# Expert outputs written to a row per token and rank, and eight ranks summed at the end, in place of a scatter that accumulates

## The chip, the cores and the metric

The kernel runs on one core of one Trainium2 chip. The metric is the device time of one execution in microseconds (us). Three runs of the kernel before gave 1620.14, 1620.84 and 1623.35 us; the median is 1620.84 us.

A core has TensorE (PE, matmuls; its weight loads are shown as PEld), VectorE (DVE), ScalarE (ACT), GpSimd (POOL) and SyncE (SP, which here only issues DMAs). The tile memory (SBUF) has 128 partitions; matmuls write to PSUM, eight banks of 128 x 512 float32.

## The reference, cut to what matters

The layer is a token mixer (four kinds of attention) and a mixture of experts. The mixer is not touched by the change. 512 tokens of width 1024 are routed to 8 of 64 experts each:

```python
_, idx = lax.top_k(jnp.where(emask, choice, -jnp.inf), TOP_K)      # 8 experts per token
sel = jnp.take_along_axis(scores, idx, axis=1)
wts = sel / jnp.sum(sel, axis=-1, keepdims=True) * ROUTED_SCALE
...
yb = swiglu(x_pad[tok], w_gate_e[e], w_up_e[e], w_down_e[e]) * w[:, None]   # per expert
acc = acc.at[tok].add(yb)                                          # summed per token
...
x = layer_norm(ALPHA * x + shared + routed, ln2_g, ln2_b)
```

So each token's output is the sum of eight weighted expert outputs, a shared expert's output and the scaled residual, and then a second layer norm. There are 512 x 8 = 4096 pairs of token and expert, 64 per expert on average.

## The kernel before, in words

The program is written by hand for each engine, with semaphores between them. It has four stages: the mixer (to about 690 us), the output projection with first norm, router and shared expert (to about 820 us), the loop over the 64 experts (to 1580 us), and the final sum with the second norm.

The router makes a table `info[:, t, e, :]` per token tile t: the token number minus 65536 (`UNUSED`) and the token's weight for expert e. `pos` holds the slot of each token in each expert. For an expert there are 128 slots. DVE compares the slot numbers with `pos` (`mark_slots`), which gives a one-hot matrix, and PE multiplies it with `info` (`slots`, four matmuls, accumulated in bank I). The result is, per slot, a token number and a weight; an empty slot gives 0. `rows_of` on DVE adds 65536 and writes two row numbers: `rows_u[:, b, 0:1]` for the gather (an empty slot is 65536, out of bounds, and is skipped), and `rows_u[:, b, 1:2]` for the scatter, cut down by `min` to a spare row 512 + slot for an empty slot.

The expert loop runs four experts per turn of a hardware loop. GpSimd gathers the tokens' rows of `x1_d` (DRAM) to `x_slots`; PE turns them (L852), multiplies by the gate and up weights (L773), turns the hidden values, and multiplies by the down weights in three products of split float32 (L786, L787, L790). ACT and DVE scale half of the result each with the slots' weights to `y_slots` (L1079, L1421), and GpSimd scatters `y_slots` with an indirect DMA that accumulates (`compute_op=ALU.add`) to `acc_d[yb]`, one of two buffers of 640 rows in DRAM. GpSimd clears both buffers before the loop (L1543). SP loads each expert's 2 MB of gate and up weights and 1 MB of down weights one expert ahead, as the buffers come free.

The order on GpSimd in the loop is: gather for expert e+2 (needs `rows_made`, and the turned slots of e), then scatter of e (needs both halves of `y_slots`). `rows_out[b]` counts the scatters of each buffer.

After the loop, SP waits for `rows_out[0]` and issues four loads of 512 KB from `acc_d[0]`, then waits for `rows_out[1]` and issues four more (L552). DVE adds `acc[0]` to the base (`mT_nat(t)`, which already holds residual and shared expert; L1475), then per token tile t `total(t)` adds `acc[1]` (L1460) and takes mean and variance, and `scale(t)` normalises and multiplies by `ln2`'s gain (L1470, L1471). GpSimd takes the root (L1507) and adds the bias (L1594), and SP stores the tile (L555). The order on DVE is total(0), total(1), scale(0), total(2), scale(1), total(3), scale(2), scale(3). PE does nothing after the loop.

If an expert has more than 128 tokens, a slow branch handles the rest (`if n > P`); it isn't taken here, the profile has 64 scatters and 66 gathers.

Of the kernel before, what the change touches and what calls it, by code (L numbers as in the profile page):

```python
# [30 lines left out]
ALU = mybir.AluOpType  # L31
# [39 lines left out]
X_PARTS = 4  # L71
W_OUT_AFTER = N_PROJ + 26
# [103 lines left out]
def build(nc, a, out):  # L176
# [9 lines left out]
    with ctx:  # L186
# [40 lines left out]
        ov_slot = sb("ov_slot", [P, P])  # L227

# [55 lines left out]
        info, o = carve(region2, o, (QT, N_EXP + 2, 2))  # L284
# [5 lines left out]
        ln2, o = carve(region2, o, (2, D))  # L290
# [5 lines left out]
        acc = [w.rearrange("p a b -> p (a b)").rearrange("p (a b) -> p a b", a=QT) for w in w_gu]  # L296
# [24 lines left out]
        acc_d = [nc.dram_tensor(f"acc_d{b}", (SEQ + P, D), F32).ap() for b in range(2)]  # L321
# [97 lines left out]
        acc_in = [[sem(f"acc_in{b}_{t}") for t in range(QT)] for b in range(2)]  # L419
# [14 lines left out]
        def _(sp):  # L434
# [113 lines left out]
            sp.wait_ge(y_out1, 3 * QT)  # L548
            for b in range(2):
                sp.wait_ge(rows_out[b], 16 * (N_EXP // 2 + 1))  # L550
                for t in range(QT):
                    sp.dma_start(acc[b][:, t, :], acc_d[b][t * P:(t + 1) * P, :]).then_inc(acc_in[b][t], 16)  # L552
# [8 lines left out]
        def _(pe):  # L561
# [232 lines left out]
            def slots(j, b):  # L794

                pe.wait_ge(onehot_made, j + 1)
                pe.wait_ge(rows_made, j)
                for t in range(QT):
                    mm = nc.tensor.matmul(PS[:, I_BANK, 0:2], onehot[:, b % 2, t, :],  # L799
                                          info[:, t, bass.ds(j, 1), :].rearrange("p a b -> p (a b)"),  # L800
                                          start=(t == 0), stop=(t == QT - 1))
                mm.then_inc(slots_done, 1)
# [84 lines left out]
            with pe.If(n > P):  # L887
                pe.sem_inc(ov["y"], 1)
                with pe.Fori(1, SEQ // P) as c:
                    with pe.Fori(0, N_EXP) as e:  # L890
                        j = (c - 1) * N_EXP + e
                        pe.wait_ge(ov["oh"], j + 1)
                        for t in range(QT):
                            mm = nc.tensor.matmul(PS[:, I_BANK, 0:2], onehot[:, 0, t, :],
# [24 lines left out]
                        mm.then_inc(ov["y"], 1)  # L919

# [181 lines left out]
        def _(dve):  # L1102
# [173 lines left out]
            def route(t):  # L1276
# [20 lines left out]
                s = sel[:, t, :]  # L1297
                link(nc.vector.tensor_tensor_reduce(rt64[:, 3, :], s, score[:, :], 1.0, 0.0, ALU.mult, ALU.add,
# [3 lines left out]
                link(nc.vector.tensor_scalar(info[:, t, 0:N_EXP, 1], rt64[:, 3, :], wsum[:, 1:2], ROUTED_SCALE,  # L1302
                                             ALU.mult, ALU.mult))

            def slots_of(t):
# [15 lines left out]
                                         ALU.add))  # L1321
            first_norm(0)
# [45 lines left out]
            def rows_of(b, done):  # L1368
                nc.vector.tensor_copy(w_slot[:, b, :], PS[:, I_BANK, 1:2])
                row = PS[:, I_BANK, 0:1]  # L1370
                nc.vector.tensor_scalar(rows_u[:, b, 0:1], row, UNUSED, None, ALU.add)
                nc.vector.tensor_scalar(rows_u[:, b, 1:2], row, UNUSED, tok_row[:, QT:QT + 1], ALU.add, ALU.min)\  # L1372
                    .then_inc(done, 1)
# [111 lines left out]
        def _(pool):  # L1485
# [60 lines left out]
            last_row = pool.to_reg(SEQ + P - 1)  # L1546
# [96 lines left out]
```

## Time and profile before

| | before |
|---|---|
| median of the runs | 1620.84 us |
| profiled execution, its own time | span 1620.6 us from first to last instruction |
| PE busy | 1415.9 us, 87% of the span |
| DVE / ACT / POOL busy | 43% / 30% / 22% |
| moved by DMA | 319.95 MB, of it 55.60 MB on GpSimd's queue |
| HBM | read 290.21 MB, written 46.92 MB |

The page gives for each engine the busy time, then the span in 40 slices of 40.5 us, then DMA queues, the chain of work that ended last (each piece followed back to what released it), groups of instructions by line, and DMA issues. A busy share is an average over the whole span; the rows further down are taken from single stages. PEclk is the granted clock of TensorE as a share of full speed: 1.00 is 2.4 GHz and 0.50 is 1.2 GHz. A float32 matmul appears as two records (for 512 columns, two of about 0.43 us at full clock).

### The profile page before, as it was taken

What the parts mean: (1) busy time and instruction counts of PE and PEld (TensorE: products, weight loads), DVE (VectorE), ACT (ScalarE), POOL (GpSimd) and SP (SyncE); (2) the same over time, 40 slices, a digit from 0 to 9 for tenths busy, and PEclk for the clock granted to TensorE, in tenths of its full rate; (3) what the DMA queues carried; (4) which work ended last, traced back from release to release, by engine and by line L of the source; (5) the groups of instructions that cost most, each with busy time, mean ns of one, the idle gap of its engine ahead of it and who ended that gap; (6) DMA issues with size and microseconds to landing.
All of it is one profiled execution on the core that took longest, in us unless ns stands there. A gap on an engine that the chain in (4) does not pass through costs nothing.

```text
span 1620.6 us, 20567 instructions
## 1 busy us (share of the span) xinstructions
PE 1415.9 (87%) x7132; PEld 1143.1 (71%) x7132; DVE 701.0 (43%) x1620; ACT 487.3 (30%) x983; POOL 354.8 (22%) x236
## 2 busy tenths in 40 slices
PE   8500399999999899997899999999999999999990
PEld 5500389966666567645778888888888888888880
DVE  3000010156466555556444444545444444544446
ACT  4000132333333232101033433434343433434330
POOL 3000132222123234301011222212122221222224
PEclk9755699999999999997999999999999999999995
DMA  4222511111111114234269999999999999999974
GB/s 150 25 25 36 160 66 65 50 50 65 33 50 49 49 66 185 80 142 190 110 225 323 351 322 341 328 334 336 322 349 312 342 333 335 334 320 344 325 237 140
DMA packets 64768, 319.95 MB, mean 197 GB/s; under 512 B 10652, under 2 KB 10780, under 8 KB 56404
## 3 DMA queue, kind: packets, MB, share of 16 engines
q1 hardware_dynamic: 44692, 263.76, 43.4%
q0 software_dynamic: 20032, 55.60, 16.2%
q8 instruction: 28, 0.46, 0.1%
q14 instruction: 16, 0.13, 0.0%
HBM read 290.21 MB, written 46.92 MB: 208 GB/s over the span
## 4 chain that ended last, share of the span: by engine, by line
PE 81%; SPq 8%; DMA 5%; DVE 4%; issue 1%; ACT 1%; POOL 0%; POOLq 0%; DVEq 0%; ACTq 0%
PE PS L773 27%; PE PS L604 15%; PE PS L786 5%; SPq L467 4%; PE PS L787 4%; PE PS L852 4%; PE PS L790 4%; PE PS L730 3%; PE PS L799 3%; PE PS L712 3%; SPq L471 3%; PE PS L660 3%; PE PS L683 2%; DMA ring<-in_w_proj 2%; DMA slots<-x_d,rows_u 2%; PE PS L671 2%
## 5 line engine op out<-in xcount | busy, mean ns | idle before, releaser
L773 PE MATMUL PS<-region,slots 128*128 128x256 f32 x2048 | 454.0, 380 | 1.4 <-ACT slots L1053 1.4
L773 PEld LDWEIGHTS PS<-region,slots 128*128 128x128 f32 x2048 | 389.7, 190 | 57.0 <-issue 1.6
L1515 POOL TENSOR_TENSOR w_lo<-ring,w_hi 128x1024 fp32r<-128x1024 f32 x54 | 128.3, 2377 | 453.0 <-ACT w_hi L935 453.0
L604 PE MATMUL PS<-x_hi,w_hi 128*128 128x512 f32 x368 | 102.4, 422 | 125.2 <-ACT w_hi L935 125.2
L1551 POOL DMA_INDIRECT slots<-x_d,rows_u x66 | 68.9, 1044 | 606.6 <-DVE rows_u L1372 597.1
L604 PEld LDWEIGHTS PS<-x_hi,w_hi 128*128 128x128 f32 x368 | 69.4, 197 | 142.4 <-issue 129.4
L1168 DVE CUSTOM_DVE_ANT_0 region<-PS,region 128x128 f32<-128x128 f32 (+1 forms) x64 | 30.6, 478 | 309.8 <-PE PS L660 307.8
L1341 DVE TENSOR_TENSOR wd_lo<-region,wd_hi 128x1024 fp32r<-128x1024 f32 x130 | 153.5, 1222 | 23.9 <-ACT wd_hi L1033 23.9
L1033 ACT ACTIVATE wd_hi<-region 128x1024 fp32r<-128x1024 f32 x130 | 129.5, 1048 | 0.0
L1024 ACT ACTIVATE slots<-PS 128x128 f32<-128x128 f32 x136 | 37.9, 279 | 302.3 <-PE PS L773 302.3
L786 PE MATMUL PS<-wd_hi,hT_hi 128*128 128x512 f32 x272 | 119.5, 439 | 3.1 <-ACT hT_hi L1028 3.1
L1326 DVE TENSOR_TENSOR slots<-PS,slots 128x128 f32<-128x128 f32 x136 | 39.2, 288 | 190.7 <-ACT slots L1024 190.7
L1557 POOL DMA_INDIRECT acc_d<-slots,rows_u x64 | 103.2, 1613 | 52.9 <-DVE slots L1421 39.0
L787 PE MATMUL PS<-wd_lo,hT_hi 128*128 128x512 f32 x272 | 107.0, 394 | 0.0
L935 ACT ACTIVATE w_hi<-ring 128x1024 fp32r<-128x1024 f32 x54 | 56.7, 1049 | 140.6 <-DMA ring<-in_w_proj 139.8
L604 PE MATMUL PS<-x_hi,w_lo 128*128 128x512 f32 x376 | 95.5, 396 | 0.0
L604 PE MATMUL PS<-x_lo,w_hi 128*128 128x512 f32 x368 | 91.9, 392 | 0.0
L1334 DVE TENSOR_TENSOR hT_lo<-PS,hT_hi 128x128 fp32r<-128x128 f32 x136 | 38.9, 286 | 121.5 <-ACT hT_hi L1028 121.5
L979 ACT ACTIVATE region<-region,nmax 128x128 f32<-128x128 f32 (+3 forms) x80 | 43.6, 546 | 149.5 <-DVE nmax L1168 149.2
L790 PE MATMUL PS<-wd_hi,hT_lo 128*128 128x512 f32 x272 | 84.6, 392 | 0.0
L1053 ACT ACTIVATE slots<-PS 128x512 f32<-128x512 f32 x130 | 70.7, 596 | 42.3 <-PE PS L852 42.3
L1079 ACT ACTIVATE slots<-PS,w_slot 128x512 f32<-128x512 f32 x64 | 44.0, 688 | 128.3 <-PE PS L790 128.3
(175 smaller groups left out, 2142.6 us busy)
## 6 DMA issues: line engine op xcount, KB each, us to landing
region<-in_w_gu SPq DMA_DIRECT2D x64, 2048.0 KB, 9.9
region<-in_w_down_e SPq DMA_DIRECT2D x64, 1024.0 KB, 7.7
ring<-in_w_merge SPq DMA_DIRECT2D x32, 640.0 KB, 3.8
ring<-in_w_proj SPq DMA_DIRECT2D x22, 512.0 KB, 3.4
acc_d<-slots POOLq DMA_DIRECT2D x2, 2560.0 KB, 19.4
region<-in_w_out SPq DMA_DIRECT2D x1, 4096.0 KB, 13.9
region<-acc_d SPq DMA_DIRECT2D x8, 512.0 KB, 5.0
bias_d<-region SPq DMA_DIRECT2D x3, 1280.0 KB
```

The costliest lines, as they stand in the source:

```text
L467: sp.dma_start(bias_d[4 * g:4 * g + 4], dist_bias[4 * g:4 * g + 4, :].unsqueeze(1) .broadcast_to([4, P, 640])).then_inc(bias_io, 16)
L604: mm = nc.tensor.matmul(PS[:, bank, :], (w_hi, w_hi, w_lo)[i][:, n % HALVES, c, :], (x_hi, x_lo, x_hi)[i][:, c, :], start=(i == 0 and c == 0),
L773: mm = nc.tensor.matmul(PS[:, G_BANK + half, 0:F], xs(c), w[:, c, half * F:(half + 1) * F], start=(c == 0), stop=(c == KT - 1))
L786: nc.tensor.matmul(PS[:, bank + n, :], hh, wd_hi[:, half, cols], start=(half == 0), stop=False)
L787: nc.tensor.matmul(PS[:, bank + n, :], hh, wd_lo[:, half, cols], start=False, stop=False)
L790: mm = nc.tensor.matmul(PS[:, bank + n, :], hl, wd_hi[:, half, n * 512:(n + 1) * 512], start=False, stop=(half == 1))
L1033: nc.scalar.activation(wd_hi[:, half, :], w_dn[b][:, half, :], ACT.Copy).then_inc(wd_hi_made, 1)
L1053: ins = nc.scalar.activation(x_slotsT[:, b % 2, 4 * h:4 * h + 4, :], PS[:, X_BANK + h, :].rearrange("p (c n) -> p c n", c=4), ACT.Copy)
L1341: nc.vector.tensor_tensor(wd_lo[:, half, :], w_dn[b][:, half, :], wd_hi[:, half, :].bitcast(F32), ALU.subtract).then_inc(wd_lo_made, 1)
L1515: nc.gpsimd.tensor_tensor(wl, w, wh.bitcast(F32), ALU.subtract).then_inc(w_lo_made, 1)
L1551: pool.indirect_dma_start(x_slots[:, xb, :], None, x1_d, bass.IndirectOffsetOnAxis(ap=rows_u[:, b, 0:1], axis=0), bounds_check=last_tok, o ...
L1557: pool.indirect_dma_start(acc_d[yb], bass.IndirectOffsetOnAxis(ap=rows_u[:, b, 1:2], axis=0), y_slots[:, yb, :], None, bounds_check=last_r ...
```

## The change: what it does

- The output of an expert is no longer accumulated in DRAM. There is one tensor `y_d` of 8 x 512 rows of 4 KB. The row for a token and an expert is rank x 512 + token, the rank being the expert's place (0 to 7) among the token's chosen experts.
- The rank comes from a running sum over the token's selection (one scan per token tile) and a multiply-add that puts rank x 512 + token - 65536 in a new column of `info`. The `slots` matmuls give three columns where they gave two, and `rows_of` writes both row numbers with one instruction. An empty slot's row number is now out of bounds for the scatter too, and is skipped.
- The scatter is a plain write (no `compute_op`). The clearing of `acc_d` is gone; a write of 16 columns to a small tensor stands in its place, so that the semaphore counts stay.
- At the end SP waits for all scatters of both buffers and then reads all of `y_d`: eight loads of 2 MB (half the ranks of a token tile each) into four buffers `parts`, the fifth and later ones as DVE and PE release a buffer.
- Of a part's four ranks DVE adds two to `mT_nat(t)`, and PE sums the other two, over both parts of a tile, in two PSUM banks by matmuls with the identity. DVE then adds the two banks.
- `ln2` shares its place with `ln1`; it is loaded after `ln1`'s last use as before.

The core of the diff, the declarations left out:

```diff
@@ final loads, SP
             sp.wait_ge(y_out1, 3 * QT)
+            sp.wait_ge(y_done, QT + N_EXP)
             for b in range(2):
                 sp.wait_ge(rows_out[b], 16 * (N_EXP // 2 + 1))
-                for t in range(QT):
-                    sp.dma_start(acc[b][:, t, :], acc_d[b][t * P:(t + 1) * P, :]).then_inc(acc_in[b][t], 16)
+            y_ranks = y_d.rearrange("(r t p) d -> t p r d", r=TOP_K, p=P)
+            for n in range(2 * QT):
+                t, half = divmod(n, 2)
+                if n >= PARTS:
+                    sp.wait_ge(dve_summed, n - PARTS + 1)
+                    sp.wait_ge(pe_summed, n - PARTS + 1)
+                sp.dma_start(parts[n % PARTS], y_ranks[t, :, 4 * half:4 * half + 4, :]).then_inc(parts_in[n % PARTS], 16)
@@ slots(j, b), PE
-                    mm = nc.tensor.matmul(PS[:, I_BANK, 0:2], onehot[:, b % 2, t, :],
+                    mm = nc.tensor.matmul(PS[:, I_BANK, 0:3], onehot[:, b % 2, t, :],
@@ end of PE's program
+            pe.wait_ge(y_out0, N_EXP + 1)
+            pe.wait_ge(y_out1, N_EXP + 2 * QT)
+            for n in range(2 * QT):
+                t, half = divmod(n, 2)
+                pe.wait_ge(parts_in[n % PARTS], 16 * (n // PARTS + 1))
+                if t >= 2 and half == 0:
+                    pe.wait_ge(sums_taken, t - 1)
+                for r in (2, 3):
+                    for h in range(2):
+                        mm = nc.tensor.matmul(PS[:, 2 * (t % 2) + h, :], ident[:, :],
+                                              parts[n % PARTS][:, r, h * 512:(h + 1) * 512],
+                                              start=(half == 0 and r == 2), stop=(half == 1 and r == 3))
+                mm.then_inc(pe_summed, 1)
@@ route(t), DVE
+                link(nc.vector.tensor_tensor_scan(rt64[:, 0, :], s, s, 0.0, ALU.add, ALU.bypass))
+                link(nc.vector.tensor_scalar(info[:, t, 0:N_EXP, 1], rt64[:, 0, :], float(SEQ), tok_off[:, t:t + 1],
+                                             ALU.mult, ALU.add))
@@ rows_of, DVE
-                nc.vector.tensor_copy(w_slot[:, b, :], PS[:, I_BANK, 1:2])
-                row = PS[:, I_BANK, 0:1]
-                nc.vector.tensor_scalar(rows_u[:, b, 0:1], row, UNUSED, None, ALU.add)
-                nc.vector.tensor_scalar(rows_u[:, b, 1:2], row, UNUSED, tok_row[:, QT:QT + 1], ALU.add, ALU.min)\
-                    .then_inc(done, 1)
+                nc.vector.tensor_copy(w_slot[:, b, :], PS[:, I_BANK, 2:3])
+                nc.vector.tensor_scalar(rows_u[:, b, 0:2], PS[:, I_BANK, 0:2], UNUSED, None, ALU.add).then_inc(done, 1)
@@ total(t), DVE
-                dve.wait_ge(acc_in[1][t], 16)
-                link(nc.vector.tensor_tensor(v, v, acc[1][:, t, :], ALU.add))
+                for n in (2 * t, 2 * t + 1):
+                    dve.wait_ge(parts_in[n % PARTS], 16 * (n // PARTS + 1))
+                    for r in range(2):
+                        link(nc.vector.tensor_tensor(v, v, parts[n % PARTS][:, r, :], ALU.add))
+                    dve.sem_inc(dve_summed, 1)
+                dve.wait_ge(pe_summed, 2 * t + 2)
+                bank = 2 * (t % 2)
+                link(nc.vector.tensor_tensor(v, v, PS[:, bank:bank + 2, :].rearrange("p a b -> p (a b)"), ALU.add))
+                dve.sem_inc(sums_taken, 1)
@@ after scale, DVE
-            for t in range(QT):
-                dve.wait_ge(acc_in[0][t], 16)
-                link(nc.vector.tensor_tensor(mT_nat(t), mT_nat(t), acc[0][:, t, :], ALU.add))
@@ before the loop, POOL
-                pool.dma_start(acc_d[b].rearrange("(t p) d -> p t d", p=P),
-                               y_slots[:, b, :].unsqueeze(1).broadcast_to([P, QT + 1, D])).then_inc(rows_out[b], 16)
+                pool.dma_start(pad_d[b], y_slots[:, b, 0:16]).then_inc(rows_out[b], 16)
@@ scatter, POOL
-                pool.indirect_dma_start(acc_d[yb], bass.IndirectOffsetOnAxis(ap=rows_u[:, b, 1:2], axis=0),
+                pool.indirect_dma_start(y_d, bass.IndirectOffsetOnAxis(ap=rows_u[:, b, 1:2], axis=0),
                                         y_slots[:, yb, :], None,
-                                        bounds_check=last_row, oob_is_err=True, compute_op=ALU.add).then_inc(done, 16)
+                                        bounds_check=last_row, oob_is_err=False).then_inc(done, 16)
```

On DVE the last part of the program, after the expert loop, stood so before (mT is the base that becomes the output, `region` holds the loaded sums and the norm's gain, mv mean and variance):

```order
L1475 TENSOR_TENSOR mT<-mT,region 128x1024 x4
L1460 TENSOR_TENSOR mT<-mT,region 128x1024
L1462 BN_STATS stats<-mT 128x6 x2
L1464 BN_AGGR mv<-stats 128x2
L1465 TENSOR_SCALAR mv<-mv 128x1
L1460 TENSOR_TENSOR mT<-mT,region 128x1024
L1462 BN_STATS stats<-mT 128x6 x2
L1464 BN_AGGR mv<-stats 128x2
L1465 TENSOR_SCALAR mv<-mv 128x1
L1470 TENSOR_SCALAR mT<-mT,mv 128x1024
L1471 TENSOR_TENSOR mT<-mT,region 128x1024
```

And the same place of the changed kernel, whose line numbers are its own:

```order
L1494 TENSOR_TENSOR mT<-mT,region 128x1024 x4
L1498 TENSOR_TENSOR mT<-mT,PS 128x1024
L1501 BN_STATS stats<-mT 128x6 x2
L1503 BN_AGGR mv<-stats 128x2
L1504 TENSOR_SCALAR mv<-mv 128x1
L1494 TENSOR_TENSOR mT<-mT,region 128x1024 x4
L1498 TENSOR_TENSOR mT<-mT,PS 128x1024
L1501 BN_STATS stats<-mT 128x6 x2
L1503 BN_AGGR mv<-stats 128x2
L1504 TENSOR_SCALAR mv<-mv 128x1
L1509 TENSOR_SCALAR mT<-mT,mv 128x1024
L1510 TENSOR_TENSOR mT<-mT,region 128x1024
```

The four adds ahead of the first tile are gone, and each tile has five adds where it had one; the norm's instructions and their order are the same. On PE the program ended with the branch of the expert loop; the changed one has one group more at its end (`ident` is the identity, `region` the loaded parts):

```order
L905 REGISTER_ALU
L905 COMPARE_AND_BRANCH
L904 REGISTER_ALU
L904 COMPARE_AND_BRANCH
L902 UNCONDITIONAL_BRANCH
L946 MATMUL PS<-region,ident 128x512 x32
L187 UNCONDITIONAL_BRANCH
```

These are four matmuls for each of the eight parts.

## Rows read from the trace of the kernel before

**Rows 1.** Page, busy tenths in 40 slices of the span.

```profile
PE   8500399999999899997899999999999999999990
DMA  4222511111111114234269999999999999999974
```

**Rows 2.** Busy by stage, mid-loop: five engines busy and count, PEclk, DMA share, GB/s.

```profile
1300.00:1400.00 100.00, 99.88 (x530) 87.08 (x528) 45.87 (x108) 39.22 (x77) 21.04 (x16) 1.00 0.99 330
```

**Rows 3.** Chain that ended last, loop: gate and up of experts 2 and 63.

```profile
847.73 6.91 PE PS L773 x32
...
1567.82 6.91 PE PS L773 x32
```

**Rows 4.** Waits in the loop, 836 to 1580 us: total, times, longest.

```profile
PEld PS L852 <- DMA slots<-x_d,rows_u: 3.3, 8, 0.7
PE PS L852 <- DMA slots<-x_d,rows_u: 0.4, 1, 0.4
```

**Rows 5.** Line of the gather (L1551), issue to landing, all 66.

```profile
DMA to landing us min/median/max: 2.2/6.3/7.5
```

**Rows 6.** Line of the scatter (L1557), issue to landing, all 64.

```profile
DMA to landing us min/median/max: 6.1/7.7/9.2
```

**Rows 7.** Chain that ended last, after the loop: start, us, what.

```profile
1579.62 0.76 DVE slots L1421
1580.43 0.55 issue
1581.21 7.10 DMA acc_d<-slots,rows_u
1588.32 3.65 DMA region<-acc_d
...
1605.08 1.15 DVE mT L1460
1606.25 1.30 DVE stats L1462 x2
...
1614.27 2.38 POOLq L186
```

**Rows 8.** Stretches (columns of rows 2): `w_out` load; PE restarts; final loads.

```profile
623.00:627.00 4.00, 4.00 (x17) 2.70 (x15) 0.76 (x2) 1.43 (x2) 0.00 (x0) 1.00 1.03 422
781.00:791.00 10.00, 6.93 (x40) 5.32 (x38) 3.92 (x13) 0.83 (x3) 0.00 (x0) 1.00 0.01 2
792.00:798.00 6.00, 6.00 (x18) 5.10 (x19) 1.54 (x5) 0.00 (x0) 2.14 (x2) 0.50 0.32 87
799.00:807.00 8.00, 7.21 (x33) 5.63 (x32) 1.66 (x6) 1.00 (x4) 0.00 (x0) 1.00 0.00 0
1584.00:1585.00 1.00, 0.00 (x0) 0.00 (x0) 0.96 (x2) 0.00 (x0) 0.00 (x0) 0.50 1.07 94
1589.00:1590.00 1.00, 0.00 (x0) 0.00 (x0) 0.00 (x0) 0.00 (x0) 0.00 (x0) 0.50 0.81 123
1591.00:1595.00 4.00, 0.00 (x0) 0.00 (x0) 2.80 (x6) 0.00 (x0) 0.00 (x0) 0.50 1.00 398
```

**Rows 9.** Timeline after the loop, DVE: start, us, instruction.

```profile
1580.93 5.00 DVE L1475 TENSOR_TENSOR mT<-mT,region 128x1024 f32<-128x1024 f32 x4 [0.56 <-issue]
1599.85 1.22 DVE L1460 TENSOR_TENSOR mT<-mT,region 128x1024 f32<-128x1024 f32 x1
1605.00 1.22 DVE L1460 TENSOR_TENSOR mT<-mT,region 128x1024 f32<-128x1024 f32 x1
```

**Rows 10.** Chain, 690 to 860 us: projection of a tile, shared expert's gate and up.

```profile
708.99 13.79 PE PS L730 x32
793.49 9.42 PE PS L773 x32
807.23 6.92 PE PS L773 x32
```

**Rows 11.** Groups of instructions by line, 690 to 900 us.

```profile
L1254 DVE SCALAR_TENSOR_TENSOR region<-x_nat,PS 128x1024 f32<-128x1024 f32 x4 | 4.9, 1222 | 23.2 <-PE PS L730 23.2
L1272 DVE TENSOR_TENSOR_SCAN region<-region 128x64 f32<-128x64 f32 x4 | 1.2, 292 | 0.1
L1302 DVE TENSOR_SCALAR region<-region,wsum 128x64 f32<-128x64 f32 x4 | 1.0, 257 | 0.1
```

**Rows 12.** Page, GpSimd's DMA queue: packets, MB, share of 16 engines.

```profile
q0 software_dynamic: 20032, 55.60, 16.2%
```

More of the change, by code:

```diff
@@ L71 @@
 X_PARTS = 4
+PARTS = 4
 W_OUT_AFTER = N_PROJ + 26
@@ L227, in build @@
         ov_slot = sb("ov_slot", [P, P])
+        tok_off = sb("tok_off", [P, QT])
         attention = ExitStack()
@@ L283, in build @@
         ln1, o = carve(region2, 0, (2, D))
-        info, o = carve(region2, o, (QT, N_EXP + 2, 2))
+        info, o = carve(region2, o, (QT, N_EXP + 2, 3))
         pos, o = carve(region2, o, (QT, N_EXP + 2))
@@ L289, in build @@
         w_dn0, o = carve(region2, o, (FT, D))
-        ln2, o = carve(region2, o, (2, D))
+        _, o = carve(region2, o, (2, D))
         assert o >= RING * SLOT + KT * D, o
@@ L295, in build @@
         x1, o = carve(region2, o, (QT, D))
-        acc = [w.rearrange("p a b -> p (a b)").rearrange("p (a b) -> p a b", a=QT) for w in w_gu]
+        ln2 = ln1
+        parts = [carve(region2, RING * SLOT + j * 4 * D, (4, D))[0] for j in range(PARTS)]
+        assert RING * SLOT + PARTS * 4 * D <= o, o
         onehot, o = carve(region2, o, (2, QT, P))
@@ L320, in build @@
         x1_d = nc.dram_tensor("x1_d", (SEQ, D), F32).ap()
-        acc_d = [nc.dram_tensor(f"acc_d{b}", (SEQ + P, D), F32).ap() for b in range(2)]
+        y_d = nc.dram_tensor("y_d", (TOP_K * SEQ, D), F32).ap()
+        pad_d = [nc.dram_tensor(f"pad_d{b}", (P, 16), F32).ap() for b in range(2)]
         S_BANK, T_BANK, O_BANK, C_BANK = 0, 2, 4, 6
@@ L418, in build @@
                                           "hturn", "hT", "y", "yout", "out", "turns")}
-        acc_in = [[sem(f"acc_in{b}_{t}") for t in range(QT)] for b in range(2)]
+        parts_in = [sem(f"parts_in{j}") for j in range(PARTS)]
+        dve_summed = sem("dve_summed")
+        pe_summed = sem("pe_summed")
+        sums_taken = sem("sums_taken")
         scaled = sem("scaled")
@@ L893, in _ @@
                         for t in range(QT):
-                            mm = nc.tensor.matmul(PS[:, I_BANK, 0:2], onehot[:, 0, t, :],
+                            mm = nc.tensor.matmul(PS[:, I_BANK, 0:3], onehot[:, 0, t, :],
                                                   info[:, t, bass.ds(e, 1), :].rearrange("p a b -> p (a b)"),
@@ L1301, in route @@
                 link(nc.vector.reciprocal(wsum[:, 1:2], wsum[:, 0:1]))
-                link(nc.vector.tensor_scalar(info[:, t, 0:N_EXP, 1], rt64[:, 3, :], wsum[:, 1:2], ROUTED_SCALE,
+                link(nc.vector.tensor_scalar(info[:, t, 0:N_EXP, 2], rt64[:, 3, :], wsum[:, 1:2], ROUTED_SCALE,
                                              ALU.mult, ALU.mult))
@@ L1321, in _ @@
                                          ALU.add))
+            link(nc.vector.tensor_scalar(tok_off[:, :], tok_row[:, 0:QT], -UNUSED - SEQ, None, ALU.add))
             first_norm(0)
@@ L1542, in _ @@
             for b in range(2):
-                pool.dma_start(acc_d[b].rearrange("(t p) d -> p t d", p=P),
-                               y_slots[:, b, :].unsqueeze(1).broadcast_to([P, QT + 1, D])).then_inc(rows_out[b], 16)
+                pool.dma_start(pad_d[b], y_slots[:, b, 0:16]).then_inc(rows_out[b], 16)
             last_tok = pool.to_reg(SEQ - 1)
-            last_row = pool.to_reg(SEQ + P - 1)
+            last_row = pool.to_reg(TOP_K * SEQ - 1)
             def gather(b, xb, done):
```

## The prediction

> **What bounds the kernel now.** I read the slices first [rows 1]: from slice 22 to the end of the loop PE and the DMA engines both stand at nine tenths, so I asked which of the two sets the pace. In mid-loop PE is busy 99.88 of 100 us at full clock, with the DMA engines at 0.99 and 330 GB/s [rows 2]. A share of 0.99 on the DMA side would look like a bound, but a bound is what others wait for. From expert 2 to expert 63 the gate and up products start 720.09 us apart, 61 periods of 11.80 us [rows 3], and in the whole loop PE and its weight loads waited for a DMA 3.7 us in nine places, always for a gather [rows 4]. No row shows it waiting for weights. So the loop is PE's, and all that lighter DMA traffic can give back in it is those 3.7 us.
>
> The end is another regime. PE's last product releases DVE's half of `y_slots` at 1579.62; the last scatter is issued at 1581.21 and lands at 1588.32, the first of the last four loads takes 3.65 us more, and from there DVE's adds and norms run to the end at 1620.6 [rows 7]. From 1579.6 to 1620.6 are 41.0 us in which PE is idle. The changed part of the end is on this chain with no cover.
>
> **The change, part by part.** The sum is made against the profiled execution's 1620.6 us; the median of the runs, 1620.84, is 0.2 above.
>
> *Router.* Two DVE instructions more per token tile, a scan of 64 columns (0.29 us) and a tensor-scalar (0.26 us) [rows 11], each with a chained wait of 0.03: 0.6 us. For three of four tiles PE has products of tens of us ahead and DVE waits for it (23.2 us before L1254) [rows 11]. The fourth tile's routing precedes the base of tile 0 and the hidden values of tile 1, for which PE waits: +0.6 us. The offset column and wider `info` are made while DVE waits for the projection: nothing. If that cover were gone, 0.3 us.
>
> *Clearing.* It moved 5.2 MB on GpSimd's queue before the loop, where nothing in the chain waited for it: 0. It and the scatters of 128 rows are most of 55.60 MB [rows 12]: 5.2 + 16.8 (4096 gathered rows) + 33.6 (64 x 128 x 4 KB). Afterwards 33.6 MB remain.
>
> *Loop.* A scatter of on average 64 rows without reading the destination replaces one of 128 rows with it; DVE's `rows_of` is one instruction shorter, so a gather starts some 0.1 us earlier; `slots` computes three columns where it had two, in the same four matmuls. Gathers land 2.2 us after issue at best and 6.3 in the median [rows 5]. With less in the queues ahead of them they land sooner, and the nine waits should go: -3.7 us, between 0 and -3.7. What is late next is PE itself, so no more than that comes.
>
> *Last scatter.* Not shown in the trace: a scatter that neither accumulates nor writes empty slots. Bounds: 7.1 us from issue to landing as now [rows 7], within the 6.1 to 9.2 us of all 64 [rows 6], and 2.2 us, the fastest gather, which moves about as many rows in the other direction with idle queues [rows 5]. I take 3.2, near the gather, with 1 us for writing DRAM rather than SBUF. It lands at 1584.4, 4.8 us after 1579.6. The Trainium skill, "DMA: Bandwidth & Descriptors", section on the anatomy of one DMA, fits a GpSimd DMA as 2.0 us plus bytes over 436 GB/s, an estimate of 2.6 us for 0.26 MB; by it the sum would be 0.6 us lower.
>
> *Reading eight ranks.* 4096 rows of 4 KB are 16.78 MB, where 2.1 MB were left to read after the last scatter. The rate is the term that matters most. The final loads of 4 KB rows ran at 398 GB/s with DVE adding beside them, and the load of `w_out`, which like the new loads takes from each partition rows far apart, at 422 [rows 8]. I take 410: 40.9 us. Lower bound 38.0 us (442 GB/s would be a twentieth above the faster row); upper bound 50.8 us, at the loop's 330 GB/s [rows 2]. Around it: the first bytes flowed about 1.5 us after the scatter's landing (half-filled window from 1589 to 1590 [rows 8]), and I put 0.9 us for the completion. The last part lands 43.3 us after the scatter. Four loads are in flight and each refill needs one buffer, so SP's refills wait behind about 15 us of queued traffic and cost nothing if DVE and PE use a part within that.
>
> *DVE at the end.* A tile's period was 1605.00 - 1599.85 = 5.15 us with one add in it; now five adds, four of 1.25 us more [rows 9], so 10.15, and the add from PSUM is like L1254's 1.22 us [rows 11]. The loads bring a tile in 10.2 us. It is a draw: DVE keeps up, but can't regain time lost at the start.
>
> *PE at the end.* Four float32 matmuls of 512 columns per part. The projection's 32 records took 13.79 us [rows 10], 0.43 each, two per matmul: 3.45 us per part at full clock, 6.9 at half. A part arrives every 5.1 us. The clock stands at 0.50 from 1584 on because PE idles [rows 8], so the first part is summed at half speed. Earlier such a restart ran fully busy at 0.50 from 792 to 798 and at 1.00 from 799 on [rows 8]; PE then needed 9.42 us for what takes 6.92 [rows 10]. So the first tile's sum comes some 3 us late; DVE has no `scale` behind total(0) and regains 2.3 of it. I put 1.5 us for what reaches the last tile.
>
> *The sum.* From the scatter's landing: 43.3 (last part) + 3.6 (PE's two ranks of it, and the hand-over) + 1.5 = 48.4 us until DVE's last PSUM add starts. From the start of the last L1460 to the end were 1620.6 - 1605.1 = 15.5 us [rows 7], the same instructions. So 4.8 + 48.4 + 15.5 = 68.7 us after 1579.6, where it was 41.0: +27.7. With the loop and router: 1620.6 + 27.7 - 3.7 + 0.6 = 1645.2, and 0.2 for the median: **1645.4 us**, 1.5% slower.
>
> **The rivals.**
>
> *A. PE's clock doesn't hold at the end.* With 3.45 us of work per 5.1 us PE is busy about two thirds. For it: from 781 to 791 it was busy 6.93 of 10 us and then stood at 0.50 [rows 8]. Against it: those were mostly small matmuls, and at half speed PE would be busy all the time, which brought the clock back at 798. If only the last part meets half speed, +3.4 us: 1649. If the clock stayed at half throughout, eight parts of 6.9 us from the first landing (7.5 us after the scatter) end at 62.7 rather than 48.4: 1660. The Trainium skill, "TensorE: Matmul & The Clock Gate", section on HAM oscillation, says that when each burst of matmuls is shorter than the wait for its data the array starts every burst cold; by that rule this loop alternates, and the time is the first of the two.
>
> *B. The ranks are read more slowly.* For it: in the loop the rate was 330 GB/s with full queues [rows 2]. Against it: much of that traffic was GpSimd's, and plain loads ran at 398 to 422. At 330: 50.8 us, +9.9: 1655. The Trainium skill, "DMA: Bandwidth & Descriptors", section on latency and other measured facts, warns that streams whose partitions lie 2 MiB apart fall to about three quarters of full rate. Here ranks are 2 MiB apart and partitions 4 KB, so the rule doesn't bite by its words; if it did, 13.6 us and 1659.
>
> *C. The scatter is as slow as before and the gathers wait on.* That is the change not doing what it says: skipped rows and no accumulation cheapen nothing. 7.1 instead of 3.2, and no gain of 3.7: 1653. Against it: the gather also skips empty slots and lands in 2.2 us at best.
>
> *D. Not slower.* The scatters would have to slow PE itself in the loop, through SBUF or PSUM, so that lighter scatters shorten each period. The point from which it decides is 24.6 us over 64 experts, 0.38 us each. Against it: PE's records in the loop (6.91 us for 32) are as short as those of the shared expert at 807, where no scatter ran (6.92) [rows 3, 10]. It would give 1620 or less.
>
> **How the numbers follow.** Forecast 0.53, A 0.2, B 0.13, C 0.11, D 0.02, the rest 0.01. The lower end: 1645.4 less 2.9 for a rate of 442, 1.0 for the scatter and 1.5 for the late first tile is 1640; I go to 1639. The upper end takes in A's and B's larger values: 1660. A difference under 0.2% (3.2 us) can't be told from none here. Only D reaches faster or the same: faster 0.01, same 0.01, slower 0.98.
>
> **What would show it.** Right: loop periods of 11.75 us with no wait for gathers; a last scatter landing in 2 to 4 us; eight loads at 400 GB/s or more, their stretch about 41 us; DVE waiting on loads or on PE's sums for tiles 1 to 3; GpSimd's queue at 34 MB. Wrong: DMA idle between the final loads (then buffers, not the rate, bound them), clock 0.50 beyond the first 8 us of PE's sums, or a loop shorter than before by more than 4 us.

## The result and the profile after

| | before | after |
|---|---|---|
| median of four runs | 1622.03 us | 1654.78 us |
| lowest to highest | 1620.14 to 1623.35 | 1653.51 to 1655.05 |
| profiled execution, span | 1620.6 us | 1651.8 us |
| GpSimd's DMA queue | 55.60 MB | 33.61 MB |

The changed kernel is slower: the ratio is 1.0197, with a 95% interval of 1.0185 to 1.021. Forecast were 1645.4 us and a range of 1639 to 1660, slower with a chance of 0.98. The direction held, and so did what bounds the loop and what lies behind it; one term of the end, DVE's pace, was wrong. The number was 9 us low (7 against the profiled span). The ratios in this document are the record's estimates from all runs; they differ from the quotients of the medians by up to 0.0008.

The chain of work that ended last, in the changed kernel, from the last expert to the end (start, us, what; L1498 is DVE's add from PSUM, L1494 its adds of loaded ranks, L946 PE's sums):

```profile
849.87 6.91 PE PS L788 x32
...
1568.21 6.91 PE PS L788 x32
...
1580.02 0.76 DVE slots L1453
...
1581.61 3.23 DMA y_d<-slots,rows_u
...
1586.44 22.50 DMA region<-y_d
1608.98 3.71 PE PS L946 x8
1612.71 1.23 DVE mT L1498
...
1617.78 1.14 DVE mT L1494
1618.95 3.26 DVE mT L1494
...
1624.98 1.23 DVE mT L1498
...
1637.24 1.23 DVE mT L1498
...
1646.35 2.37 POOLq L187
```

Read it against [rows 3, 7]. In the loop 61 periods took 718.34 us where they took 720.09: 1.75 us came back. DVE's last half of `y_slots` is released at 1580.02 (before: 1579.62), and from there to the end are 71.8 us where they were 41.0. The two stretches and a start of the loop that is 2.0 us later (837.97 against 835.96) make up the 31.2 us between the spans.

The scatter lands 3.23 us after its issue (before 7.10), and GpSimd's queue moves what the count of rows gave. After the scatter PE and DVE wait for loads until 1612.7. From there the chain never names a load again: it is DVE alone up to GpSimd's last bias adds, and for tiles 2 and 3 one of DVE's adds takes 3.26 us where its neighbours take 1.2.

Busy by stretch (PE, PEld, DVE, ACT, POOL with their counts, then PEclk, DMA share, GB/s) of the changed kernel:

```profile
1586.00:1587.00 1.00, 0.00 (x0) 0.00 (x0) 0.00 (x0) 0.00 (x0) 0.00 (x0) 0.50 0.94 197
...
1587.00:1628.00 41.00, 28.65 (x56) 11.28 (x56) 27.04 (x30) 0.00 (x0) 5.78 (x3) 0.85 1.02 409
1593.00:1599.00 6.00, 6.00 (x7) 2.42 (x8) 3.42 (x3) 0.00 (x0) 0.00 (x0) 0.50 1.02 410
1600.00:1636.00 36.00, 25.32 (x56) 9.72 (x54) 30.30 (x32) 0.00 (x0) 10.09 (x5) 1.00 0.86 342
...
1628.00:1629.00 1.00, 0.04 (x1) 0.00 (x0) 0.97 (x3) 0.00 (x0) 0.86 (x1) 1.00 0.74 299
```

The DMA engines moved 409 GB/s through the whole stretch. Not all of it were loads: the store of tile 0's output, 0.52 MB issued at 1621.14, passed among them. PE's clock was at half speed until 1599 and at full speed from 1600 on, although PE was busy only 25.32 of those 36 us.

The timeline of the same kernel shows who was beside the long add (start, us, instruction, idle before it and its releaser):

```profile
1612.71 1.22 DVE L1498 TENSOR_TENSOR mT<-mT,PS 128x1024 f32<-128x1024 f32 x1 [1.27 <-PE PS L946]
...
1617.70 7.13 DVE L1494 TENSOR_TENSOR mT<-mT,region 128x1024 f32<-128x1024 f32 x4
1617.86 3.26 POOL L1629 TENSOR_TENSOR mT<-mT,region 128x1024 f32<-128x1024 f32 x1 [0.93 <-DVE mT L1510]
...
1624.98 1.22 DVE L1498 TENSOR_TENSOR mT<-mT,PS 128x1024 f32<-128x1024 f32 x1
...
1629.41 3.70 PE L946 MATMUL PS<-region,ident 128*128 128x512 f32 x8 [1.38 <-DMA region<-y_d]
```

Four adds together take 7.13 us, not 5.0. GpSimd's add of the bias for the tile before (L1629) begins at 1617.86, while DVE's first add runs to 1618.9; it ends at 1621.12, and DVE's second add, begun at 1618.95, ends at 1622.2. Each engine seems to have stood still while the other worked. Tile 1's PSUM add still waits 1.27 us for PE; tile 2's waits for nothing.

Before the change the same pair met. The timeline of the kernel before, after the loop:

```profile
1600.02 3.26 POOL L1594 TENSOR_TENSOR mT<-mT,region 128x1024 f32<-128x1024 f32 x1 [0.93 <-DVE mT L1471]
1601.11 1.29 DVE L1462 BATCH_NORM_STATS2 stats<-mT 128x6 f32<-128x512 f32 x2
...
1602.74 1.08 DVE L1470 TENSOR_SCALAR mT<-mT,mv 128x1024 f32<-128x1024 f32 x1
...
1610.31 2.84 POOL L1594 TENSOR_TENSOR mT<-mT,region 128x1024 f32<-128x1024 f32 x1 [0.93 <-DVE mT L1471]
1610.98 3.24 DVE L1471 TENSOR_TENSOR mT<-mT,region 128x1024 f32<-128x1024 f32 x1
```

In the first group GpSimd's add began behind DVE's add of 1599.85 and was the one that waited (3.26 us, alone 2.34). Then DVE's statistics ran beside it at their usual 1.29 us, and DVE lost only 0.27 us, in L1470. In the last group GpSimd was ahead, and DVE's gain took 3.24 us.

### The profile page after: what moved, and what is told of

Read it like the earlier page. It is cut to its first block, busy times and chain, and to the rows that moved or that the text cites. A ratio compares the mean times of both kernels' runs of the same rounds, so it can differ in the third digit from the quotient of the medians.

```text
span 1651.8 us, 20667 instructions
## 1 busy us (share of the span) xinstructions
PE 1449.2 (88%) x7196; PEld 1157.2 (70%) x7196; DVE 713.7 (43%) x1575; ACT 487.8 (30%) x983; POOL 313.4 (19%) x236
## 3 DMA queue, kind: packets, MB, share of 16 engines
q0 software_dynamic: 18784, 33.61, 5.6%
## 4 chain that ended last, share of the span: by engine, by line
PE 82%; SPq 8%; DVE 5%; DMA 4%; issue 1%; ACT 1%; POOL 0%; POOLq 0%; DVEq 0%; ACTq 0%
PE PS L788 28%; PE PS L619 15%; PE PS L801 5%; SPq L476 4%; PE PS L802 4%; PE PS L805 4%; PE PS L867 3%; PE PS L745 3%; PE PS L814 3%; PE PS L727 3%; SPq L480 3%; PE PS L675 3%; PE PS L698 2%; DMA ring<-in_w_proj 2%; PE PS L686 2%; DMA region<-y_d 1%
## 5 line engine op out<-in xcount | busy, mean ns | idle before, releaser
L1551 POOL TENSOR_TENSOR w_lo<-ring,w_hi 128x1024 fp32r<-128x1024 f32 x54 | 128.2, 2375 | 454.0 <-ACT w_hi L965 454.0
L1453 DVE TENSOR_SCALAR slots<-PS,w_slot 128x512 f32<-128x512 f32 x64 | 48.0, 751 | 78.3 <-PE PS L805 78.3
```

The source lines that it names most:

```text
L1551: nc.gpsimd.tensor_tensor(wl, w, wh.bitcast(F32), ALU.subtract).then_inc(w_lo_made, 1)
```

## Experiments

The theory: the last 25 us go at DVE's pace, and DVE's tile costs 12.27 us because one of its adds per tile is stretched by GpSimd's bias add. Its rivals: the loads bound the end, PE's slow start is what arrived, or something else stretches the add. A second question is where the loop's 1.75 us and the 3.9 us of the last scatter come from: from skipping, or from not accumulating. All medians are of timed runs; the kernel before had 1622.19, 1621.35 and 1622.36 in the three groups of runs, and each ratio is to the kernel before.

### The bias added by DVE

```diff
-                nc.vector.tensor_tensor(v, v, ln2[:, 0, :], ALU.mult).then_inc(scaled, 1)
+                link(nc.vector.tensor_tensor(v, v, ln2[:, 0, :], ALU.mult))
+                nc.vector.tensor_tensor(v, v, ln2[:, 1, :], ALU.add).then_inc(out_made, 1)
...
-                    nc.gpsimd.tensor_tensor(mT_nat(t - 1), mT_nat(t - 1), ln2[:, 1, :], ALU.add).then_inc(out_made, 1)
```

> The changed kernel with the final norm's bias added by DVE in scale(t), right behind the gain; GpSimd's four adds at the end are gone. Theory (DVE's add of two SBUF operands stands still for 2 us each time GpSimd's bias add runs beside it): all L1494 adds take 1.24 us, a tile's period on DVE falls from 12.27 us to 12.27 - 2.03 + 1.24 = 11.5, the last PSUM add starts 1.6 us earlier, and the end loses the stalled gain (2.0) and GpSimd's last add: about 3.3 us less than the changed kernel's 1654.8, 1651.5. Rival (the slow add comes from the loads that write the same memory, or from PE's reads): one add per tile stays near 3.3 us, the period grows to 13.5, and the time is 1655 to 1656.

Measured: 1651.17 us (1650.37 to 1652.47), ratio 1.0181 [1.0164, 1.0198]. All sixteen adds of loaded ranks (least, median and longest ns, first and last start) are short, where the changed kernel has 1216/1225/3255:

```profile
L1494 DVE TENSOR_TENSOR mT<-mT,region x16: 1216/1225/1227, 1593.5 to 1635.1; 128x1024 f32<-128x1024 f32 x16
```

Tile 1 to tile 2 is 11.50 us (PSUM adds at 1613.11 and 1624.61), which is 12.27 less the 2.0 of stretching plus the 1.2 of an instruction more on DVE. From tile 2 to tile 3 are 11.90 us, since DVE stands 0.5 us before its third add there for no reason that the profile shows. The theory's number came within 0.4 us. DVE has one instruction more per tile, and yet from its last half of `y_slots` to its last PSUM add are 56.2 us where they were 57.2: it was not DVE's work but the sharing with GpSimd that cost. The loads wrote the same memory and PE read it as before, so neither stretched the add. The rest of the gain is the end behind the last PSUM add, 12.6 us where it was 14.6.

### No bias at all

The bias is left out of the output, on both engines: the same edit without DVE's add, and the gain releases the store.

> The changed kernel with the final bias add left out (so the output lacks ln2's bias). Theory (GpSimd's adds stall DVE): DVE's tile period falls to 10.2 us, which is the loads' pace, the last PSUM add starts when PE is done with the last part, some 4.1 us earlier, and the end is 4.3 us shorter: about 1646.5. Then the end is bound by the loads at about 410 GB/s. Rival (DVE is slowed by the loads or by PE): one slow add per tile stays, only the end is shorter: about 1650.5.

Measured: 1645.13 us (1644.83 to 1648.29), ratio 1.0149 [1.0132, 1.0165]. DVE's PSUM adds in the timeline:

```profile
1612.73 1.22 DVE L1498 TENSOR_TENSOR mT<-mT,PS 128x1024 f32<-128x1024 f32 x1 [1.27 <-PE PS L946]
...
1622.97 1.22 DVE L1498 TENSOR_TENSOR mT<-mT,PS 128x1024 f32<-128x1024 f32 x1
...
1633.20 1.22 DVE L1498 TENSOR_TENSOR mT<-mT,PS 128x1024 f32<-128x1024 f32 x1
```

The period is 10.24 us, and in the chain of this kernel the last part's load ends at 1629.39 with PE's 3.71 us behind it, which gives 1633.20. This is the end as it had been forecast: loads, PE, DVE level with them. What the bias add beside DVE costs ahead of the last PSUM add is the 4.0 us between 1633.20 and 1637.24 (DVE's last half of `y_slots` began at 1580.06 here and at 1580.02 there).

### Half of the last four loads

The last four loads bring two ranks of a part, 1 MB where it was 2, so the output lacks two ranks for parts of tiles 2 and 3.

```diff
+                lo, hi = (0, 4) if n < PARTS else (1, 3)
+                sp.dma_start(parts[n % PARTS][:, lo:hi, :],
+                             y_ranks[t, :, 4 * half + lo:4 * half + hi, :]).then_inc(parts_in[n % PARTS], 16)
```

> The changed kernel with the last four of the eight final loads cut to two of four ranks, 1 MB each (the other two ranks of tiles 2 and 3 are summed from what the buffer held, so the output lacks them); DVE's and PE's work is the same. Theory (from tile 1 on the end is bound by DVE, the loads run ahead of it): the last load lands 10 us earlier, and the time changes by less than 0.7 us, 1654 to 1655; one add per tile still takes 3.3 us. Rival (the end is bound by the loads, as the prediction had it): up to 10 us less, 1645 to 1648. Rival (the loads slow DVE's adds): the slow adds of tile 3 fall to 1.24 us, about 2 us less.

Measured: 1654.76 us (1653.66 to 1655.59), ratio 1.0202 [1.0185, 1.0219]. PE's sums, which had stood apart by 1.4 us of waiting, run together:

```profile
1609.77 17.43 PE L948 MATMUL PS<-region,ident 128*128 128x512 f32 x40 [1.26 <-DMA region<-y_d]
```

A quarter of the bytes is gone and nothing is gained: DVE's PSUM adds are 12.27 and 12.26 us apart, as in the changed kernel. The loads do not bound the last two tiles.

### PE kept busy before the first part

```diff
+            for j in range(14):
+                nc.tensor.matmul(PS[:, Y_BANK + 1, :], ident[:, :], xT[:, j % KT, :], start=True, stop=True)
```

> The changed kernel with 14 matmuls of 512 columns put on PE between the end of the loop and the first part, into a bank that nobody reads, so that PE doesn't idle for 12 us. Theory: the granted clock stays at 1.00, the first part is summed in 3.7 us instead of 6.9, the first PSUM add starts about 1.5 us earlier; but tile 1 waits for its own load and DVE sets the pace after it, so the end doesn't move: 1654.8 within 0.7 us. Rival (the half-speed start is what makes the end late, as the prediction's 1.5 us): 1.5 to 3 us less.

Measured: 1653.89 us (1652.14 to 1654.41), ratio 1.0193 [1.0176, 1.021]; from 1584 to 1594 PE is busy throughout at clock 1.00. The chain of this kernel:

```profile
1581.74 0.76 DVE slots L1455
...
1588.15 21.68 DMA region<-y_d
...
1613.62 1.23 DVE mT L1500
...
1638.14 1.23 DVE mT L1500
```

DVE's first PSUM add comes 1.5 us earlier (21.6 us after DVE's release at 1581.74, where it was 23.1), but the last only 0.8 us (56.4 against 57.2), and the median is 0.9 below the changed kernel's, where 0.7 was allowed. Even that 0.8 is not PE's: tile 1 is released by the fourth load, which ended 28.1 us after the release here and 28.9 in the changed kernel. In the changed kernel PE waited 0.74 us before its third group of sums and 1.4 before the fourth, so its late start had gone before tile 1.

### The same add on GpSimd, elsewhere

The bias is left out of the output; GpSimd makes an add of the same size on buffers that nothing else uses by then (`x_slots`, with `ln2` as second operand). It is released by a semaphore step of DVE just behind the gain, not by the gain itself, so DVE's next instruction starts some 0.25 us later.

> The changed kernel with the final bias left out of the output as in a_no_bias, but with GpSimd doing four adds of the same size at the same times, on buffers that nobody else uses then. Theory (DVE's add with two SBUF operands and GpSimd's add shut each other out, whatever memory they touch): one add per tile takes 3.3 us again, the tile's period is 12.3 us, and as only GpSimd's last add is off the path the time is 3.5 us under the changed kernel's, 1651. Rival (they meet only in the tile that both work on): all adds take 1.24 us and the time is a_no_bias's, 1645.

Measured: 1653.66 us (1649.8 to 1654.73), ratio 1.0194 [1.0179, 1.021]; profiled span 1648.1.

```profile
1613.79 2.34 POOL L1631 TENSOR_TENSOR slots<-slots,region 128x1024 f32<-128x1024 f32 x1 [0.99 <-DVEq L1511]
1613.90 7.21 DVE L1494 TENSOR_TENSOR mT<-mT,region 128x1024 f32<-128x1024 f32 x4 [0.24 <-DVE mT L1510]
...
1639.12 2.34 POOL L1631 TENSOR_TENSOR slots<-slots,region 128x1024 f32<-128x1024 f32 x1 [0.99 <-DVEq L1511]
...
1639.23 2.77 DVE L1509 TENSOR_SCALAR mT<-mT,mv 128x1024 f32<-128x1024 f32 x1 [0.25 <-DVE mT L1510]
```

GpSimd began 0.11 us ahead, took its own 2.34 us, and DVE's four adds took 7.21. The outputs share no address, so it isn't two engines writing one tile. The order decides who waits: whoever begins second stands still. At 1639.23 even a tensor-scalar of DVE, 0.81 us elsewhere, took 2.77 behind GpSimd's add; in the changed kernel, where DVE began first (1642.23, GpSimd at 1642.39), it took 0.81. The Trainium skill, "SBUF — State Buffer", section "Who interferes with whom", says that a DVE instruction with two SBUF inputs contends with a GpSimd instruction that reads SBUF, as an exclusive lock; the trace agrees, with these numbers. From DVE's last half of `y_slots` (1575.76) to the end are 72.3 us, in the changed kernel 71.8, and a tile takes DVE 12.67 us where it took 12.27, with the 0.25 us of the semaphore step in it: all of the cost is there with other buffers. The profiled execution is short only since its loop began 4.3 us earlier. The median is 2.7 us above the theory's 1651, which had left out the semaphore steps and that GpSimd's last add (1643.47) still stands at the end of the program.

### Skipping alone, and not accumulating alone

First the kernel before with nothing but the skip: the scatter uses the gather's row numbers, out of bounds for an empty slot, and still accumulates; DVE makes one row number instead of two. It moves 38.86 MB on GpSimd's queue instead of 55.60.

```diff
-                pool.indirect_dma_start(acc_d[yb], bass.IndirectOffsetOnAxis(ap=rows_u[:, b, 1:2], axis=0),
+                pool.indirect_dma_start(acc_d[yb], bass.IndirectOffsetOnAxis(ap=rows_u[:, b, 0:1], axis=0),
...
-                                        bounds_check=last_row, oob_is_err=True, compute_op=ALU.add).then_inc(done, 16)
+                                        bounds_check=last_tok, oob_is_err=False, compute_op=ALU.add).then_inc(done, 16)
```

> The kernel before with one part of the change alone: empty slots skipped by the scatter (the accumulation in two buffers, the clearing and the end stay). Theory (the loop is bound by PE, skipping only takes away the waits for gathers and shortens the last scatter): the loop gives 1.5 to 3.7 us, the last scatter lands 2 to 3 us sooner than its 7.1: about 1617, 5 us less than before. Rival (accumulating costs the same whatever the number of rows, and what took the waits away was the missing accumulation): within 1.5 us of 1622.

Measured: 1621.88 us (1619.1 to 1623.65), ratio 1.000 [0.999, 1.001]. The scatter, issue to landing of all 64:

```profile
DMA to landing us min/median/max: 6.2/6.9/8.6
```

The least is nearly what it was, the median 0.8 us less [rows 6], and the last one is 6.89 where it was 7.10. The expectation of 1617 fell. The total can't tell a small gain from none, though. In the profile 61 periods of the loop took 718.8 us, 1.3 less, but the loop began at 837.26, 1.3 later than before the change, and PE was 1.0 us late already at 761.76, ahead of anything that this edit touches. The other kernel with the skip, further down, began its loop as late (837.34). Why is open.

Then the kernel before without accumulation, all 128 rows written (`compute_op` left out; the output lacks most of the sum):

> The kernel before with the other part alone: scatters of all 128 rows without accumulation (rows written over each other, so the output lacks most of the experts' sum). Theory: the last scatter lands 3 us sooner, the loop's waits go partly: 1617 to 1619. Rival (the number of rows is what counts): the landing stays near 7 us, and the time within 1 us of 1622.

Measured: 1616.70 us (1614.88 to 1618.14), ratio 0.9968 [0.9955, 0.9981]. The same view:

```profile
DMA to landing us min/median/max: 3.4/4.0/8.1
```

The last one landed after 4.17 us. And the changed kernel with the skip undone, empty slots written to spare rows:

```diff
-                nc.vector.tensor_scalar(rows_u[:, b, 0:2], PS[:, I_BANK, 0:2], UNUSED, None, ALU.add).then_inc(done, 1)
+                nc.vector.tensor_scalar(rows_u[:, b, 0:1], PS[:, I_BANK, 0:1], UNUSED, None, ALU.add)
+                nc.vector.tensor_scalar(rows_u[:, b, 1:2], PS[:, I_BANK, 1:2], UNUSED, pad_row[:, b % 2:b % 2 + 1], ALU.add, ALU.min)\
+                    .then_inc(done, 1)
```

> The changed kernel with empty slots written too, to 256 spare rows behind the eight ranks. Theory (both parts of the relief are small): the last scatter lands in 4 us instead of 3.2, the loop loses up to 1.5 us: 1655 to 1657. Rival (skipping is free of effect once nothing accumulates): within 0.5 us of 1654.8.

Measured: 1654.07 us (1653.85 to 1654.82), ratio 1.0197 [1.0179, 1.0216]; GpSimd's queue at 50.37 MB, the landing 3.4/4.0/7.1 us, the last 3.37, where the changed kernel has 3.2/4.0/6.6 and 3.23. The expected 1655 to 1657 didn't come. The three agree on the larger part: accumulating costs about 3 us per scatter, with all rows or with half (least 6.1 and 6.2 us against 3.4 and 3.2). Once nothing accumulates, skipping the empty half is worth nothing that these runs can tell; while the scatter accumulates it lowers the median by 0.8 us. The loop's 61 periods took 718.8 us with the skip alone, 718.0 without accumulation and 718.1 here, against 720.1 and 720.5 in two more kernels (the next two sections) that left the scatter alone. The waits for gathers, 3.7 us [rows 4], fell to 1.3, 0.3 and none, and no edit gets the loop below 718. The kernel before shows why so little came back:

```profile
836.00:1580.00 744.00, 742.94 (x3906) 648.97 (x3904) 354.77 (x820) 294.76 (x568) 167.10 (x127) 1.00 0.98 327
```

PE itself was idle for only 1.06 of these 744 us; most of the 3.7 us were waits of its weight loads (PEld) beside a matmul that still ran.

### The rank's two instructions

The kernel before with the scan and the tensor-scalar, their result unused:

```diff
+                link(nc.vector.tensor_tensor_scan(rt64[:, 0, :], s, s, 0.0, ALU.add, ALU.bypass))
+                link(nc.vector.tensor_scalar(rt64[:, 1, :], rt64[:, 0, :], float(SEQ), tok_row[:, t:t + 1],
+                                             ALU.mult, ALU.add))
```

> The kernel before with the two DVE instructions of the rank in each token tile's routing, their result unused. Theory: 0.55 us of longer wait of PE in the fourth tile's routing makes the granted clock fall to 0.50 earlier than without them (784 to 788 us at about 0.6 rather than 1.00), so the loop starts 2 us later than the 835 to 837 us of the kernels without the rank: about 1.5 to 2 us slower than before. Rival (the later start is run-to-run scatter or comes from the missing clearing): the clock is 1.00 from 784 to 788, the loop starts at 836 to 837, and the time is within 0.7 us of before.

Measured: 1624.30 us (1622.87 to 1627.73), ratio 1.0019 [1.001, 1.0028]: 1.9 us by the medians, 3.1 by the ratio. The place where the theory put it, a lower clock from 784 to 788, was wrong: it was 1.00 there. The chain has it later:

```profile
822.81 10.18 PE PS L773 x32
...
837.87 6.91 PE PS L773 x32
```

The products of expert 0 took 10.18 us, in the kernel before 8.70 (from 822.38), and from 826 to 830 the clock was 0.63 here and 1.00 there. So 0.4 us of DVE reached PE, and the clock came back later by a further 1.5. But over the profiled executions of all kernels expert 1's products start at 837.8 us on average with these instructions (eight executions, 833.7 to 839.9) and at 836.1 without (five, 834.8 to 837.3, the two latest those with the skip). Of a term of this size one profile says little, and what the clock adds to the 0.55 us of work stays open.

### The kernel before with the bias of the last tiles on DVE

The lock stood in the kernel before too. For tiles 2 and 3 DVE adds the bias itself, for tiles 0 and 1 GpSimd does; nothing else is changed.

```diff
+                if t < 2:
+                    nc.vector.tensor_tensor(v, v, ln2[:, 0, :], ALU.mult).then_inc(scaled, 1)
+                else:
+                    link(nc.vector.tensor_tensor(v, v, ln2[:, 0, :], ALU.mult))
...
+                    nc.vector.tensor_tensor(v, v, ln2[:, 1, :], ALU.add).then_inc(out_made, 1)
```

> The kernel before with empty slots skipped, and the bias of the last two token tiles added by DVE rather than GpSimd. Theory: beside the 5 us of the skipping, DVE adds 2.5 us of work at the end, but its last gain (3.24 us beside GpSimd's add) falls to 1.24 and GpSimd's last add with its hand-over (3.5 us) goes: 3 us less, about 1614. Rival (the 3.24 us are not GpSimd's doing): 1 us less, about 1616.

This was first run with the skip: 1617.79 us (1616.74 to 1619.94), ratio 0.9979 [0.9968, 0.999], beside the skip alone at 1.000. The expected 1614 had counted 5 us for the skip, which didn't come; the 3 us of the bias came as 4.1 by the medians. Then by itself:

> The kernel before with the bias of the last two token tiles added by DVE, and nothing else. Theory (skipping empty slots had no part in the gain of b_skip_bias_dve): 3 to 3.5 us faster than before, 0.998. Rival (half of that gain was the skipping): 1.5 us.

Measured: 1619.64 us (1617.24 to 1620.85), ratio 0.9982 [0.9973, 0.9991], 2.7 us faster than the kernel before by the medians (3 to 3.5 were expected). The end of its chain (L1474 the gain, L1477 the bias):

```profile
1608.73 1.24 DVE mT L1474
...
1609.99 1.22 DVE mT L1477
...
1611.97 1.24 DVE mT L1474
...
1613.23 1.23 DVE mT L1477
```

The last gain takes 1.24 us where it took 3.24, and GpSimd's last add no longer stands behind it. Of the complete kernels these two are the only ones that beat both the kernel before and the changed one; their intervals overlap.

## Why the prediction was right, and where it was off

The measured time lies in the stated range, but in its upper part, and that part was there for rivals A and B. Neither of them happened: 1655 was B's time, for slower reads. What took the time was not among the rivals. That the number fell inside is in part luck, and so is that two smaller errors hid some 2.4 us of the one below.

- **What bounds the kernel.** Right. The loop is PE's, and only the end moved by much: 30.8 of the 31.2 us.
- **Last scatter.** 4.8 us after DVE's release were forecast, 4.8 measured. The prediction gave two reasons, no accumulation and half the rows. The price goes with the accumulation; with it gone, all 128 rows landed after 3.37 us and half of them after 3.23.
- **Reading eight ranks.** A rate of 410 GB/s was forecast, 409 measured. The eighth load ended 44.6 us after the scatter, 43.3 forecast. The first bytes flowed 1.7 us after the landing (1.5 forecast), and the last load's end came 0.7 us after its last bytes (0.9). Between them passed the 16.78 MB and tile 0's store of 0.52 MB, which the sum had left out: at this rate 1.3 us, an estimate from the bytes. No run leaves the store away.
- **DVE at the end.** This is the step that failed: "It is a draw: DVE keeps up". A tile takes DVE 12.27 us, not 10.15, because one L1494 add takes 3.26 us beside GpSimd's bias add. It enters twice, between tile 1 and tile 3. The loads' 10.24 us are then never the limit for the last two tiles, as half the bytes showed, and 4.0 us are lost against the kernel without the bias. The prediction took the period 1605.00 - 1599.85 in [rows 9] from a place where GpSimd was the one that waited and DVE lost 0.27 us; the timeline of before had a 3.24 us gain (L1471) behind the bias add six microseconds later. The sign that the prediction had named, DVE waiting for loads or PE's sums for tiles 1 to 3, showed for tile 1 alone.
- **PE at the end.** 3.70 us per part and the half-speed start were as forecast. The 1.5 us that were to reach the last tile didn't: PE had caught up before the fourth part. It hid part of the step above in the sum.
- **The end behind the last add.** 14.6 us, 15.5 forecast. The 0.9 us are not the change's: from GpSimd's add at 1610.31 the kernel before took 10.3 us to its end, and the kernel before without accumulation 9.4 us for the same instructions (from 1604.32).
- **The sum.** The last PSUM add starts 52.4 us after the scatter's landing, 48.4 forecast: + 1.3 (loads and the store among them) + 4.1 (DVE against GpSimd, as 2 x 2.03) - 1.5 (PE's start) gives 52.3. With the end 0.9 shorter that is + 3.1 in the tail. The loop gave 1.75 of 3.7, and the start of the loop is 2.0 late instead of 0.6: + 2.0 and + 1.4. 1645.2 + 3.1 + 2.0 + 1.4 is 1651.7, the profiled 1651.8. That execution itself took 1653.51 us, 1.7 more than its span, where the prediction had put 0.2 for what lies around the span; it is also the fastest of the four, 1.3 below their median.
- **Loop.** The rows gave 3.7 us of waiting for gathers; with these gone only 1.75 came back (periods of 11.78 us, not 11.75), as in the three other kernels with light scatters (1.3 to 2.1). 3.3 of the 3.7 were waits of the weight loads, and PE itself was idle for 1.06 us. That a wait of a weight load is no wait of PE while a matmul still runs is argued from these rows, not tried by itself.
- **Router.** Work of 0.55 us, some 2 to 3 us measured, open as said above.
- **Rival A** (the clock doesn't hold) is out: 1.00 from 1600 on with PE busy 25.32 of 36 us. Only the first parts ran at half speed, which the forecast had. The Trainium skill's "TensorE: Matmul & The Clock Gate", section on HAM oscillation, speaks of bursts shorter than the wait; here a burst of 3.70 us stood before a wait of 1.4, so its case was not met, which the prediction could have read from its own numbers. **Rival B** is out (409 GB/s with the ranks 2 MiB apart). Its counter-argument, that much of the loop's traffic was GpSimd's, was thin: 50 MB of some 243 (744 us at 327 GB/s), a fifth. **Rival C** is out for the last scatter (3.23 us). Its doubt about the skip was well placed. **Rival D** is out: the loop gave 1.75 us where 24.6 were needed.

## What to carry to other kernels

When an engine's period in a new stage is built from durations of single instructions, look for the longest record of that form in the trace, not the median, and ask who ran beside it: a wide add on GpSimd beside a wide add on VectorE is no gain when the second is on the path. The accumulating scatter landed about 3 us later here and held GpSimd 0.6 us longer (1.59 against 1.02 us), and PE hid almost all of it; replacing it by eight rows to read moved 14.7 MB more to the one place where nothing hid them. And when reads at the end are priced, the stores that pass among them belong in the bytes. Before a change that trades work inside a covered loop for work behind it, price the part behind it first.

## What the runs showed of the hardware

- A 128x1024 float32 add on GpSimd (2.34 us alone) and one on DVE (1.22 us alone) with all operands in SBUF exclude each other: the second takes up to 3.3 us, on different buffers as well, and a DVE tensor-scalar that begins behind GpSimd's add takes 2.77 us instead of 0.81. DVE's statistics (BATCH_NORM_STATS2, one input) ran beside GpSimd's add at their usual 1.29 us. A DVE add from PSUM beside GpSimd's add was not seen.
- An indirect scatter of 4 KB rows lands 3.2 to 3.4 us after issue at best without accumulation, with 64 or with 128 rows, and 6.0 to 6.2 with it, again with either.
- PE's clock stayed at full speed from 1600 to 1636 us while PE worked in bursts of 3.70 us with 0.7 to 1.4 us between them, the last ending at 1633.1.
- A store of 0.5 MB issued while two loads of 2 MB were still to land (tile 0's) took 9.5 us from issue to landing; the other stores of the same size took 2.6.
- 409 GB/s over 41 us for loads of 4 KB rows whose four ranks lie 2 MiB apart, with one store of 0.5 MB among them; `w_out` was loaded at 422.
